# A recurrent mixer with tokens on partitions, and the output gate's matmuls among its heads

## The reference

```python
def mlstm_chunkwise(q, k, v, i_pre, f_pre):
    ...
        logw = cum[..., :, None] - cum[..., None, :] + i_[..., None, :]
        ...
        m_t = jnp.maximum(log_inter, jnp.max(logw, axis=-1))
        w_intra = jnp.exp(logw - m_t[..., None])
        ...
        sc = jnp.einsum('bhtd,bhsd->bhts', q_, k_) * w_intra
        num = jnp.einsum('bhts,bhsv->bhtv', sc, v_) + ...
        den = jnp.sum(sc, axis=-1) + ...
        h = num / jnp.maximum(jnp.abs(den), jnp.exp(-m_t))[..., None]
...
        hm = rms_norm(hm, mlstm_head_norm[l]).reshape(b, s, SZ_MV)
        hm = (jax.nn.sigmoid(m_o.astype(jnp.float32)) * hm).astype(x.dtype)
        y_mlstm = hm @ w_proj_mlstm[l]
        gates = jax.nn.sigmoid(g_pre.astype(jnp.float32)).astype(x.dtype).reshape(b, s, 2, D_MODEL)
        merged = gates[:, :, 0] * y_attn + gates[:, :, 1] * y_mlstm
```

## Time and profile before

| | us |
|---|---|
| median of 3 runs | 2506.02 (2504.4 to 2506.24) |
| profiled execution | 2507.38 |
| its span, first to last instruction | 2505.6 |
| `mo`, 8 dense groups, start to end on TensorE | 1807.6 to 1851.2 |
| `mlstm`, start to end on TensorE | 1851.2 to 1989.3 |

### The profile page before, as it was taken

One profiled execution on the slowest core, in us unless ns is written; L12 is line 12 of the kernel. 1 busy time (PEld: TensorE's weight loads), 2 busy tenths in 40 slices (PEclk: granted clock), 3 DMA queues, 4 the chain that ended last, 5 costly groups with the idle time before them and its releaser, 6 DMA issues.

```text
span 2505.6 us, 27240 instructions
## 1 busy us (share of the span) xinstructions
PE 2325.3 (93%) x11044; PEld 1869.6 (75%) x11044; DVE 822.4 (33%) x1407; ACT 914.6 (37%) x1434; POOL 913.0 (36%) x395
## 2 busy tenths in 40 slices
PE   6989879999699999769999999999998799999998
PEld 5769667767588888658888878678765587888886
DVE  4365434533533320342111021635316412211101
ACT  4624444543344432333223222643324433322321
POOL 3330142224355454444444434134421244344351
PEclk9979979999799999879999999999987899999999
DMA  4210141123133333212332323023320033233231
GB/s 145 75 51 1 49 140 51 53 83 95 49 101 93 94 107 102 68 59 84 101 96 89 110 79 93 26 80 98 93 59 1 9 95 99 91 93 94 85 117 51
DMA packets 54988, 197.92 MB, mean 79 GB/s; under 512 B 6352, under 2 KB 7248, under 8 KB 54480
## 3 DMA queue, kind: packets, MB, share of 16 engines
q1 hardware_dynamic: 52416, 188.77, 25.0%
q10 hardware_dynamic: 2448, 7.41, 0.8%
HBM read 194.06 MB, written 2.10 MB: 78 GB/s over the span
## 4 chain that ended last, share of the span: by engine, by line
PE 86%; DVE 7%; ACT 3%; issue 2%; POOL 1%; DMA 1%; ACTq 0%; DVEq 0%; SPq 0%; POOLq 0%
PE dense L675 20%; PE dense L677 19%; PE dense L676 19%; PE misc L640 3%; PE misc L642 2%; PE misc L641 2%; PE dense L660 2%; PE dense L661 2%; PE dense L662 2%; DVE em_b L2191 1%; PE dense L781 1%; PE dense L930 1%; PE dense L694 1%; POOL slot L583 1%; PE dense L695 1%
## 5 line engine op out<-in xcount | busy, mean ns | idle before, releaser
L603 POOL TENSOR_TENSOR w_lo<-raw,w_hi 128x1024 fp32r<-128x1024 f32 x349 | 851.4, 2454 | 1370.6 <-ACT w_hi L1201 1370.6
L675 PE MATMUL dense<-u_hi,w_hi 128*128 128x512 f32 x1392 | 548.5, 394 | 1.5 <-DVE slot L1760 1.1
L676 PE MATMUL dense<-u_lo,w_hi 128*128 128x512 f32 x1392 | 543.4, 390 | 0.0
L677 PE MATMUL dense<-u_hi,w_lo 128*128 128x512 f32 x1392 | 543.1, 390 | 0.0
L1201 ACT ACTIVATE w_hi<-raw 128x1024 fp32r<-128x1024 f32 x352 | 361.4, 1050 | 183.0 <-PE dense L677 101.0
L675 PEld LDWEIGHTS dense<-u_hi,w_hi 128*128 128x128 f32 x1392 | 262.2, 188 | 59.3 <-issue 2.8
L676 PEld LDWEIGHTS dense<-u_lo,w_hi 128*128 128x128 f32 x1392 | 262.2, 188 | 56.6 <-issue 2.9
L677 PEld LDWEIGHTS dense<-u_hi,w_lo 128*128 128x128 f32 x1392 | 262.1, 188 | 54.8
L677 PE MATMUL dense<-a_hi,w_lo 128*128 128x512 f32 x528 | 205.6, 389 | 0.0
L676 PE MATMUL dense<-a_lo,w_hi 128*128 128x512 f32 x528 | 205.6, 389 | 0.0
L675 PE MATMUL dense<-a_hi,w_hi 128*128 128x512 f32 x528 | 205.6, 389 | 0.0
(11 more groups left out here) (386 smaller groups left out, 3579.6 us busy)
## 6 DMA issues: line engine op xcount, KB each, us to landing
raw<-in_weights SPq DMA_DIRECT2D x352, 512.0 KB, 3.6
h<-in_x SPq DMA_DIRECT2D x4, 512.0 KB, 6.1
alibi<-in_alibi ACTq DMA_DIRECT2D x1, 2048.0 KB, 7.3
h<-in_x ACTq DMA_DIRECT2D x2, 1024.0 KB, 6.0
out<-result SPq DMA_DIRECT2D x8, 256.0 KB, 2.2
masks_in<-in_masks ACTq DMA_DIRECT2D x1, 512.0 KB, 9.1
p_raw<-in_p ACTq DMA_DIRECT2D x1, 512.0 KB, 3.4
mvb<-in_mvb ACTq DMA_DIRECT2D x1, 512.0 KB, 3.3
```

Of the source, the lines that this page charges most:

```text
L603: nc.gpsimd.tensor_tensor(w_lo[:, s % SPLITS, :, :], raw[:, s % RAWS, :, :], w_hi[:, s % SPLITS, :, :].bitcast(F32), ALU.subtract).then_in ...
L675: mm(out, hi, src_hi[:, i, :], start=(i == 0), stop=False)
L676: mm(out, hi, src_lo[:, i, :], start=False, stop=False)
L677: last = mm(out, lo, src_hi[:, i, :], start=False, stop=(i == k - 1))
```

## The change

**The numerator with tokens on partitions.** `wsc` becomes the stationary operand and the values the moving one. `mv` gets a 129th column of ones for each head, so that one matmul of 129 columns gives numerator and denominator of 128 tokens; 10 blocks make a head. The denominator is now one column, and the quotient a few instructions on 2 or 4 elements of each partition. The bound exp(-m) is transposed once to columns (`ecol`) with the gate rows (`mlstm_rows`, between `mv0` and `mv1`), and is no longer broadcast.

**The norm by accumulation.** ACT squares the numerator times its inverse denominator with the sum taken along the way (`head_root`), and makes the inverse root of 4 elements. DVE (`normed`) scales the numerator into `y_t`. Four transposes on TensorE (`turn`) bring the head back to features on partitions, and DVE multiplies by gain and gate in one instruction into `hn`, which now has a place for each head.

**One table set.** A set of ACT's function tables with Exp and Ln is loaded once; the output gate's sigmoid is made as exp(-ln(1 + exp(-x))), so that no other set is wanted in the mixer.

**The dense run inside.** Head `hd` of the mixer has group `hd` of `mo` around it: 4 of its 8 steps before `turn` and `front`, 4 behind `back`. All groups of `mo` use PSUM bank 3; the mixer's own tiles move to `misc0` to `misc3` and banks 0 to 2. `gate_m0` stands before the last `turn`, and each `gate_m` one place ahead of `proj_m`. POOL is left with `m_lo` alone.

```diff
@@ dense_layers (order of the weight stream)
+    a.append(("gate_m0", 1, 8, 0))
     for m in range(DC):
-        a += [(f"gate_m{m}", 1, 8, 0), (f"proj_m{m}", 1, 8, 0)]
+        if m + 1 < DC:
+            a.append((f"gate_m{m + 1}", 1, 8, 0))
+        a.append((f"proj_m{m}", 1, 8, 0))
...
+            bank_of[START["mo"][1] + m] = 3
+            bank_of[START[f"gate_m{m}"][1]] = 4 + m % 2
+            bank_of[START[f"proj_m{m}"][1]] = 6 + m % 2
@@ TensorE
                 def back(hd):
+                    pe.wait_ge(mws, 3 * hd + 3)
                     if hd >= 1:
-                        pe.wait_ge(meb_copied, hd)
-                        pe.wait_ge(mhn, 2 * hd)
-                    mm(misc[2][:, :], ident[0:8, hd:hd + 1].broadcast_to([8, P]), emx[0:8, :],
-                       start=True, stop=True).then_inc(mnd_done, 1)
-                    pe.wait_ge(mws, 3 * hd + 3)
+                        pe.wait_ge(y_ready, hd)
                     x = wsc[:, hd % 2, :]
-                    for dst, den in ((1, True), (0, False)):
-                        w = lambda j: ones[:, :] if den else mv[:, j, hd * P:(hd + 1) * P]
...
+                    for tt in range(NT):
+                        for j in range(tt + 1):
+                            col = block_at(j, tt)
+                            last = mm(bank[tt // 2][:, (tt % 2) * (P + 1):(tt % 2 + 1) * (P + 1)], x[:, col:col + P],
+                                      mv[:, j, hd, :], start=(j == 0), stop=(j == tt))
+                    last.then_inc(num_done, 1)
+
+                def turn(hd):
+                    pe.wait_ge(y_ready, hd + 1)
                     if hd >= 1:
-                        pe.wait_ge(head_rt, 12 + hd)
-                    mm(misc[3][:, :], ones[:, :], msq[:, :], start=True, stop=True).then_inc(head_sum, 1)
-
+                        pe.wait_ge(hn_done, hd)
+                    for tt in range(NT):
+                        last = tr(bank[2][:, tt * P:(tt + 1) * P], y_t[:, hd % 2, tt, :], ident[:, :])
+                    last.then_inc(yt_done, 1)
 
                 front(0)
-                for hd in range(MH + 1):
+                for hd in range(MH):
+                    for i in range(4):
+                        dense_part("mo", hd, i, u_hi, u_lo)
+                    if hd >= 1:
+                        turn(hd - 1)
                     if hd + 1 < MH:
                         front(hd + 1)
-                    if hd >= 1:
-                        mean_square(hd - 1)
-                    if hd < MH:
-                        back(hd)
+                    if hd == 0:
+                        pe.wait_ge(mv_done, 10)
+                    back(hd)
+                    for i in range(4, DC):
+                        dense_part("mo", hd, i, u_hi, u_lo)
+                dense("gate_m0", u_hi, u_lo)
+                turn(MH - 1)
@@ ScalarE
+            def head_root(hd):
+                rd, ms, rs = (hcol[:, hd % 2, k, :] for k in range(3))
+                act.wait_ge(den_done, hd + 1)
+                if hd >= 2:
+                    act.wait_ge(yt_done, hd - 1)
+                for tt in range(NT):
+                    ins = f(y_t[:, hd % 2, tt, :], bank[tt // 2][:, (tt % 2) * (P + 1):(tt % 2) * (P + 1) + P], ACT.Square,
+                            scale=rd[:, tt:tt + 1], accum_out=ms[:, tt:tt + 1])
+                act_link(act, ins)
+                act_link(act, f(rs, ms, ACT.Ln, bias=eps_col, scale=1.0 / P))
+                f(rs, rs, ACT.Exp, scale=-0.5).then_inc(mrt_done, 1)
+
+            def out_gate(hd):
+                x = so[:, hd, :]
+                act.wait_ge(dense_done, group_of("mo", hd))
+                ins = f(x, out_bank("mo", hd)[:, :], ACT.Exp, bias=nbmo[:, hd:hd + 1], scale=-1.0)
+                ins.then_inc(so_done, 1)
+                act.wait_ge(so_done, hd + 1)
+                act_link(act, f(x, x, ACT.Ln, bias=one_col))
+                f(x, x, ACT.Exp, scale=-1.0).then_inc(so_ready, 1)
+
+            decay(0)
             for hd in range(MH + 1):
+                if hd < MH:
+                    feed("mo", hd)
                 if hd + 1 < MH:
-                    decay_weights(hd + 1)
+                    decay(hd + 1)
+                if hd < MH:
+                    head_root(hd)
...
                 if hd >= 1:
+                    act.wait_ge(hn_done, hd)
+                    f(m_hi[:, hd - 1, :], hn[:, hd - 1, :], ACT.Copy).then_inc(mh_part, 1)
                 if hd < MH:
+                    out_gate(hd)
@@ VectorE
             def quotient(hd):
 
+                rd = hcol[:, hd % 2, 0, :]
+                dve.wait_ge(num_done, hd + 1)
+                for b in range(2):
+                    ins = STT(rd[:, 2 * b:2 * b + 2], numerator(b)[:, :, P], -1.0, ecol[:, 2 * b:2 * b + 2, hd],
+                              ALU.mult, ALU.max)
+                dve_link(dve, ins)
+                for b in range(2):
+                    ins = TT(rd[:, 2 * b:2 * b + 2], numerator(b)[:, :, P], rd[:, 2 * b:2 * b + 2], ALU.max)
+                dve_link(dve, ins)
+                v.reciprocal(rd, rd).then_inc(den_done, 1)
...
             for hd in range(MH + 1):
+                if hd >= 1:
+                    dve.wait_ge(yt_done, hd)
+                    dve.wait_ge(so_ready, hd)
+                    STT(hn[:, hd - 1, :], bank[2][:, :], V("head_norm", hd - 1), so[:, hd - 1, :], ALU.mult, ALU.mult)\
+                        .then_inc(hn_done, 1)
                 if hd + 1 < MH:
                     diagonal_in(hd + 1)
+                if hd < MH:
+                    quotient(hd)
                 if hd + 1 < MH:
                     weigh(hd + 1)
                 if hd < MH:
-                    quotient(hd)
+                    normed(hd)
```

More of the change, by code:

```diff
@@ L96, with block_at @@
 NSLABS = -(-TILES // SLAB)
+MOFF = (512, 1024, 896)
+def block_at(j, tt):
+    return j * P if tt == j else MOFF[j] + (tt - j - 1) * P
 VECS = {}
@@ L479, in build @@
         frees("rows2", r2_act, [1])
-        frees("mv0", mv_done, [1, 2, 3, 4])
-        frees("mv1", mv_done, [5, 6, 7, 8])
+        frees("mv0", mv_done, [3, 4, 5, 6])
+        frees("mv1", mv_done, [7, 8, 9, 10])
         frees("mo", so_done, [m + 1 for m in range(8)])
@@ L1078, in front @@
                     for j in range(NT):
-                        last = mm(bank[1][:, j * P:(j + 1) * P], k(j), q(j, j + 1), start=True, stop=True)
-                    for j, _, b, at_col in off:
-                        last = mm(bank[b][:, at_col:at_col + (3 - j) * P], k(j), q(j + 1, NT), start=True, stop=True)
+                        last = mm(misc[1][:, j * P:(j + 1) * P], k(j), q(j, j + 1), start=True, stop=True)
+                    for j, ps, col in ((0, 2, 0), (2, 2, 3 * P), (1, 3, 0)):
+                        last = mm(misc[ps][:, col:col + (3 - j) * P], k(j), q(j + 1, NT), start=True, stop=True)
@@ L1617, in _ @@
             feed("mv1")
-            for c in range(8):
-                after_group("mo", c)
-                f(so[:, c, :], out_bank("mo", c)[:, :], ACT.Sigmoid, bias=V("b_mo", c)).then_inc(so_done, 1)
-            act.wait_ge(r2_dve, 5)
-            f(emx[0:8, :], r_raw[0:8, :], ACT.Exp, scale=-1.0).then_inc(r2_act, 1)
-            act.wait_ge(mqk_silu, 8)
-            f(mxr, r_f[0:8, :], ACT.Copy).then_inc(r2_act, 1)
-            off = [(0, 512), (2, 896), (1, 1024)]
-            def decay_weights(hd):
+            act.wait_ge(mrow_tr, 1)
@@ L1628, in decay_weights, with decay @@
+            f(small[:, 0:32], misc[0][:, 0:32], ACT.Copy).then_inc(ac_done, 1)
+            f(small[:, 32:64], misc[0][:, 32:64], ACT.Exp, scale=-1.0).then_inc(ac_done, 1)
+            def decay(hd):
                 act.wait_ge(mb_done, hd + 1)
-                act.wait_ge(ac_done, 1)
-                act.wait_ge(mv_done, 8)
+                if hd == 0:
+                    act.wait_ge(ac_done, 2)
+                    act.wait_ge(mv_done, 10)
                 if hd >= 2:
-                    act.wait_ge(mnd_done, 3 * (hd - 1))
+                    act.wait_ge(num_done, hd - 1)
@@ L1633, in decay_weights @@
                 act.wait_ge(mdg_in, hd + 1)
                 x = wsc[:, hd % 2, :]
-                for j, at_col in off:
-                    f(x[:, at_col:at_col + (3 - j) * P], bank[0][:, (j + 1) * P:S], ACT.Exp,
+                for j in range(3):
+                    f(x[:, MOFF[j]:MOFF[j] + (3 - j) * P], misc[0][:, (j + 1) * P:S], ACT.Exp,
                       bias=acol[:, j, hd:hd + 1], scale=-1.0)
                 f(x[:, 0:S], x[:, 0:S], ACT.Exp, scale=-1.0).then_inc(mw_exp, 1)
-            decay_weights(0)
+            def head_root(hd):
[9 more added lines that the diff above has]
+                f(rs, rs, ACT.Exp, scale=-0.5).then_inc(mrt_done, 1)
@@ L1662, in _ @@
-            for m in range(DC):
-                after_group(f"gate_m{m}")
+                    out_gate(hd)
+            for m in range(DC + 1):
+                if m < DC:
+                    after_group(f"gate_m{m}")
```

(5 more changed lines are left out.)

155 lines of the change are left out of this document (64 added, 91 removed).

## The result

| | before | changed |
|---|---|---|
| median | 2505.31 us (2504.4 to 2506.24) | 2423.56 us (2421.86 to 2427.8) |
| ratio, 95% interval | | 0.9676, 0.9659 to 0.9693 |
| profiled execution, span | 2507.38, 2505.6 | 2422.05, 2420.2 |

The change makes the kernel 81.8 us faster. Forecast were 2438 us and a range from 2425 to 2458: the direction was right, the gain came out 14 us larger, and the median lies 1.4 us under the range.

The account below looks back on a forecast made before the run. It took the mixer's circle over three engines, with TensorE's float32 columns and idle time, as the bound. The stretch falls from 200.6 to 123.9 us, 76.7 saved, less 8.5 for the clock: 2438 us, range 2425 to 2458.

Parts of the forecast that it names:

- the one wait: TensorE's next group of `mo` waits for ACT to free the shared bank (`so_done`): 1.7 us idle a head, seven times.
- The stretch: First matmul of `mo` to end of `gate_m1`, holding the mixer, `gate_m0` and `proj_m0`: 200.6 us before, 132 forecast.
- The cover named for DVE, ACT and POOL: In the mixer, their work fits under TensorE's: 2.7 us of cover for `y_ready`, POOL's 2.4 us slab split in 13.7.
- TensorE's work of a head: In the mixer at full clock: dense steps, broadcast, scores, numerator, transposes and crossings sum to 12.0 us.
- DVE's part: Within the bank wait, DVE's small quotient after the numerator: five instructions in three dependent steps, 0.85 us.
- the two root steps: Within the bank wait, ACT's two steps on 4 elements at 0.264 us, with signals 0.6 us.
- the copy and the Exp: Within the bank wait, ACT's copy to `m_hi` and the Exp reading the bank: 0.636 us each, 1.4 with signals.
- the sum at full clock: `mo`, mixer, `gate_m0`, `proj_m0`, `gate_m1` together: 123.9 us where 200.6 stood, 76.7 saved.
- The clock term: In the mixer, idle times of 1.7 us partly lower TensorE's clock: 8.5 us cost, a third of 25.
- The clock falls in every head: Rival: the 1.7 us gap lowers the clock in each head of the mixer, 52 us saved, 2454 us; chance 0.20.
- No stall: Rival: ACT frees the bank of `mo` before TensorE comes, clock stays full, 2417 to 2429 us; chance 0.17.
- Only the dense run is won: Rival: the mixer's circle stays 17.3 us a head, only the 43.6 us of `mo` are saved, 2462 us; chance 0.09.

Follow-up runs that it names:

- s6: Changed kernel with the groups of `mo` in two PSUM banks in turn, transposes moved to the last scores' bank: medians 2420.4 and 2418.3 us.
- s3: Changed kernel with the four squares of each head made twice on ACT, same result: 2448.8 us.
- s1: Changed kernel with the 8 groups of `mo` ahead of the mixer again and POOL's `m_lo` behind them: 2490.2 us, ratio to before 0.995.
- s7: Changed kernel with removed columns put back on TensorE (numerator's matmuls twice, two matmuls of 512 float32 columns a head): 2459.7 us, one execution.
- s5: Kernel with `mo` ahead of the mixer, plus 16 unread filler matmuls of 512 columns ahead of each head's transposes: 2465.1 us.
- s2: Changed kernel with the output gate's first Exp, which frees the bank of `mo`, moved ahead of the inverse root and the copy to `m_hi`: 2422.9 us.
- s9: Changed kernel with two of the four dense steps ahead of the transposes moved between broadcast and scores: 2428.0 us.
- s8: Changed kernel with `mo` in two PSUM banks and two dense steps of each head moved between broadcast and scores: 2419.1 us.

## Why the prediction was right or wrong

**The direction, the mechanism and the one wait were right.** The stretch is TensorE's work plus seven waits for `so_done`; TensorE waits for nothing else in it, neither slabs nor `y_t`. No table load stands among the heads. The cover named for DVE, ACT and POOL holds: DVE waits for TensorE, ACT for DVE, POOL for ACT.

**TensorE's work of a head**, 12.0 us, was 11.8 by the period of s6, which has no waits. The numerator was inside its bounds of 2.2 to 2.5.

**The wait, term by term, was a little too long.** 1.7 us were forecast and 1.24 measured. DVE's part was 0.73 (priced 0.85), the four squares 1.5 (1.6), the two root steps 0.44 (0.6), the copy and the Exp 1.2 together (1.4): each price was somewhat high. The instructions of 512 columns were taken as standing end to end at 0.636 us; the Exp starts 0.52 us behind the copy. A wait of 1.24 us costs 1.5 (the third trace of the changed kernel beside the second of s6). With 11.8 us of work the period is 13.3, where 12.0 + 1.7 = 13.7 stood: 0.4 too much in each of seven heads, nearly all of the 3 us by which the sum at full clock, 123.9, was over the measured 121 (125.8 less the falls).

**The clock term failed, in size and in part in its reason.** 8.5 us were forecast, a third of 25, for idle times of 1.7 us. Three falls of 3.4 us were there, 10 us low, and a fall costs 1.6 us: 4.9 us, 3.6 less than the term. None of the three begins right behind an idle time of 1.2 us; each follows a broadcast and scores, as the falls of s6 do, where TensorE has no idle time at all. The term had no place for these. That idle times bring the clock down holds for the 2.8 us of s3. The two errors, 3 and 3.6 us, make the stretch 132.4 us for 125.8.

**The rest of the miss was no term of the sum.** The unchanged part ahead of the mixer was taken at its value in one trace, 1667.4 us for the projection's start, and its scatter at nothing; in fourteen traces of this study it lies between 1656.3 and 1667.7. The trace before stood at the late end, with 157 us at the half clock ahead of the projection where the changed kernel's had 130. 14.4 us of miss are 6.6 of the stretch, 11.1 - 0.5 of this scatter in the profiled execution, less 2.9 by which the forecast and the measured median lay off from what their profiled executions gave (1.4 and 1.5). The range had no room for such a scatter on the low side: its low end, 2425, was 13 us under the forecast, and the median of all 12 executions, 2426.7, would have lain in it. That the first median fell outside was in part the luck of the draw; that the sum of the stretch was 6.6 us too long was not.

**The rivals.** "The clock falls in every head" did not come true for this kernel, but did for the same mixer without the dense run inside (s1: 99 us low). By the Trainium skill, "TensorE: Matmul & The Clock Gate", section "A second HAM failure mode: psum-queue depth-cycling", short idle times between groups that cycle through banks make the clock swing. The traces agree for the idle times of 2.8 us in s3 (four of seven with a fall right behind them), and not for those of 1.24 us in the changed kernel, nor for the seven of 0.78 us in the `mo` run of s1, which stayed at 1.00. "No stall" named a time of 2417 to 2429 us and holds the measured one, but for another reason: there was a stall. With a second bank it came true, at 2418 to 2420. "Only the dense run is won" (2462) fails: s7 shows the removed columns to be worth 33 us of the 75.

**How the 75 us of the stretch divide.** The new form alone gives 13 (s1), the dense run inside 62 more. Of the 62, 25 are idle time of TensorE that is filled (33.6 us in s1's stretch, 8.2 in the changed kernel's), and 37 are the same 586 matmuls running faster, since the clock is up. The two parts can't be priced one by one: the removed columns count nearly in full with the dense run inside (s7); that they would count for less without it is argued, not tested. The old form with the dense run inside wasn't tried, since its tiles take all 8 banks; s7 stands in for it on TensorE alone.

## What to carry to other kernels

A circle over several engines is well filled with dense work of the same queue, and not only for the idle time: from s1 to s5 the same mixer went from a clock of 0.61 to 0.84 by matmuls that nobody reads. When a run is put inside a circle, look at who frees its PSUM bank and how late that engine comes to it; a second bank took 9 to 10 us off the stretch here, more than the 6.6 by which the forecast missed it. Before a gain of 3% is forecast to within half a per cent, take the unchanged part from more than one trace.

## What the runs showed of the hardware

- TensorE's clock fell to its half level 3.0 to 3.7 us behind the start of a broadcast and scores (3.4 us over 8 and 64 rows, with no idle time among them), in 12 of 42 passes of the changed kernel, s2 and s6 (for one, 1830.72 to 1834.21 of the changed kernel), also where TensorE did not wait in the whole stretch (s6). With two dense steps between them it fell in none of 14 passes (s9, s8). I had looked for idle times only.
- Behind an idle time of 2.8 us with dense steps on both sides (s3) the clock fell in four of seven cases, for 3.4 us each: 17 us low in a stretch of 140. Behind idle times of 0.8 us (the `mo` run of s1) and 1.2 us (the changed kernel) it did not fall: its falls there stand 5 to 7 us later, behind the next broadcast and scores.
- The same instructions, from the start to the attention's projection, took 1656 to 1668 us from one execution to the next, with 130 to 157 us of them at the half clock.
